# A hybrid decoder trunk: attention split into a projection phase and an interleaved attention, gate and output phase

## The chip, the cores and the metric

The kernel runs on one core of a Trainium2 chip. The metric is device time in microseconds (us) of one execution, median of several runs. The engines that matter are PE (TensorE: matrix products and transposes, results in PSUM), ACT (ScalarE: activations, copies), DVE (VectorE: element-wise work), POOL (GpSimd: the same, slower) and SP, whose queue issues nearly all DMA transfers. Each engine runs its own instruction list in order and waits on semaphores that other engines raise.

## What is computed

One inference step of two layers over 2048 prompt tokens and 8 sample tokens of width 1024. Layer A is a gated short convolution. Layer B is attention with its own queries against shared keys and values in three groups with (window, dilation) = (128,1), (512,4), (2048,16); 8 query heads and 2 key/value heads of width 128 per group.

```python
k, v = rope((rms_norm(x, g) @ w_kv)[keys]), (rms_norm(x, g) @ w_kv)[values]     # 3 groups x 2 heads
q, z = rope((rms_norm(x, pre) @ w_in)[: 3*8*128]), (rms_norm(x, pre) @ w_in)[3*8*128 :]
for g in range(3):                         # query t reads t - k*d, k = 0..window/d
    s = q[g] @ k[g].T * SCALE;  s = where(mask, s, -inf)
    lse[g] = logsumexp(s);      o[g] = exp(s - lse[g]) @ v[g]
alpha = softmax(lse over g)
o = sum(alpha[g] * o[g])
y = x + rms_norm((o * silu(z)) @ w_out, post)
```

With dilation d, the tokens t = r mod d form a sequence of their own. A tile is 128 query tokens of one such sequence. A query of it sees at most two blocks of 128 keys: its own and the one before. In the group with dilation 16 each sequence has just 128 tokens, so all 16 tiles have one block; in the middle group 4 of 16 have one; in the group with dilation 1 all are handled with two.

Single-precision products are made as three passes: each operand is split into a high part (a rounded copy, made by ACT) and a low part (the rest, a subtraction on DVE or POOL), and hi x hi + lo x hi + hi x lo are accumulated. A product over 1024 inputs into 512 columns thus takes 8 x 3 = 24 matmuls.

## The kernel before

`decoder_program` (L2257) runs four phases, each closed by a barrier.

1. **Convolution layer** (`conv_phases` L56 and its helpers): leaves the residual rows `h_rows` and the normalised rows `hn_rows` in DRAM. The change does not touch it.
2. **`attention_phase`** (L807), for each group in the order 0, 1, 2 and for each tile (`step`): the tile's 128 tokens are loaded in the order of the group and turned (8 transposes, with high and low parts by ACT `high` L1283 and DVE `low` L1385). They are the stationary operand of `project` (`product` L1120 to L1127): 3 banks of 512 columns (K and V, first four query heads, last four), 72 matmuls. DVE (L1409, L1410) and POOL (L1511) apply the rotary factors. Keys and queries are turned (`turn` L1110). For each half of the heads (two units a tile): `scores` (L1156 to L1158), mask and maximum on DVE (L1426, L1429), the exponent bias (L1434), `exponentials` on ACT (L1313), `turn_probs`, `values` (L1185 to L1187, the values stationary and the turned probabilities moving, 512 columns), a copy on ACT (L1321) and `turn_sums`. The function `between` places the next tile's projection in six spots of this one, so that PE has products to do while the other engines work. The 8 sample rows are projected once per group (`project_sample`). Each tile's sums, exponent bias and denominator go to DRAM as `partial`.
3. **`sample_attention_phase`** (L1551): the 8 sample tokens against the caches. Meanwhile 16 weight slices, of the gate's and of the output's matrix, are loaded and split and stay for the next phase.
4. **`attention_output_phase`** (L1880), for each token tile: tokens are loaded and turned again, the gate product (`d_z`, L2055 to L2057), Silu on ACT (L2122), merge coefficients (L2174 to L2188), `weigh` (L2147, two groups on POOL and one on DVE), sums and gating on DVE (L2200 to L2207), a turn of the gated rows, the output product (`d_out`, same lines), square sum, root (ACT L2109), `reciprocal_root` (L39) and normalising (L2163) on DVE, the residual sum on POOL (L2234).

The order of the work inside a phase is the order in which each engine's instructions are written out; there is no planner.

Of the kernel before, what the change touches and what calls it, by code (L numbers as in the profile page):

```python
# [22 lines left out]
P = 128  # L23
D = 1024
# [775 lines left out]
OMW = D + 2 * HEADS  # L800

Item = namedtuple("Item", "g i u last")


def attention_phase(nc, hn_rows, w_kv, w_q, kv_gain, q_gain, rope_rows,  # L807
                    partials, caches_out, q_sample, new_rows, newest):
# [4 lines left out]

    TILES = SEQ // P
    UN = 4
    BODIES = TILES // UN
    EACH = range(GROUPS)
    ITEMS = TILES + 1
    KW = KVW + KVW + D
    BANK_COLS = [slice(b * BANK, (b + 1) * BANK) for b in range(3)]

    def rows(w):

        step = DILATIONS[w.g]
        row_i, row_u = ((UN * P, P), (1, UN * P), (UN, 1))[w.g]
        return bass.ds(row_i * w.i + row_u * w.u, P, step=step)

    def ahead(w, k):


        u = w.u + k
        if not w.last or u < UN:
            return Item(w.g, w.i + u // UN, u % UN, w.last)  # L840
        if w.g == GROUPS - 1:
            return None
        return Item(w.g + 1, 0, None, False) if u == UN else Item(w.g + 1, 0, u - UN - 1, False)

    def exists(w, k):

        return not w.last or w.u + k < UN or w.g < GROUPS - 1

    def ordinal(w):

        return ITEMS * w.g + (0 if w.u is None else 1 + UN * w.i + w.u)

    def parity(w):

        return (ITEMS * w.g + (0 if w.u is None else 1 + w.u)) % 2

    def landed(w):

        return (ITEMS * w.g + (0 if w.u is None else 1 + w.u)) // 2 + (0 if w.u is None else UN // 2 * w.i) + 1

    def height(w):
        return NS if w.u is None else P

    def number(w):

        return TILES * w.g + UN * w.i + w.u

    def has_before(w):

        return w.g == 0 or (w.g == 1 and w.u > 0)  # L870

    def names(w):

        probs = ("a", "b") if has_before(w) else ("a",)
        tokens = ("h0", "h1") if exists(w, 2) else ()
        return ["q0", "k", "q1", *tokens, *("p0" + x for x in probs), *("p1" + x for x in probs), "o0", "o1"]

    per_body = [sum(len(names(Item(g, 0, u, False))) for u in range(UN)) for g in EACH]

    first_job = [6, 6 + BODIES * per_body[0] + 2, 6 + BODIES * (per_body[0] + per_body[1]) + 4]  # L880
    assert all(n % 2 == 0 for n in per_body)

    def job(w, name):

        before = sum(len(names(w._replace(u=v))) for v in range(w.u)) + names(w).index(name)
        return first_job[w.g] + before + per_body[w.g] * w.i, before % 2

    def run_steps(engine, g, step):

        with engine.Fori(0, BODIES - 1) as i:  # L890
            for u in range(UN):
                step(Item(g, i, u, False))
        for u in range(UN):
            step(Item(g, BODIES - 1, u, True))

    def sample(g):
        return Item(g, 0, None, False)

    def first(g, u):
        return Item(g, 0, u, False)  # L900

    with ExitStack() as ctx:
        def sb(name, shape, dt=F32):
            return ctx.enter_context(nc.sbuf_tensor(f"g_{name}", shape, dt))

        def ps(name, shape):
            return ctx.enter_context(nc.psum_tensor(f"g_{name}", shape, F32))

        def sem(name):
            return nc.alloc_semaphore(f"g_{name}")  # L910

        w_raw = [sb(f"w_raw{b}", [P, KW]) for b in range(2)]
        w_hi = sb("w_hi", [P, KT, KW], F32R)
        w_lo = sb("w_lo", [P, KT, KW], F32R)
        gains = sb("gains", [P, 2, KT])
        tok = [sb(f"tok{b}", [P, D]) for b in range(2)]
        ht_hi = [sb(f"ht_hi{b}", [P, KT, P], F32R) for b in range(2)]
        ht_lo = [sb(f"ht_lo{b}", [P, KT, P], F32R) for b in range(2)]
        trig = [sb(f"trig{b}", [P, 3, HD // 2]) for b in range(2)]
        rot_a = sb("rot_a", [P, 3, BANK])  # L920
        rot_b = sb("rot_b", [P, 3, BANK])

        raw = [w_raw[0][:], w_raw[1][:], *(x[:].rearrange("p b n -> p (b n)") for x in (rot_a, rot_b))]
        RAW = len(raw)
        q_rot = [sb(f"q_rot{n}", [P, BANK]) for n in range(KVH)]
        kv_rows = [sb(f"kv_rows{b}", [P, 2 * KVW]) for b in range(2)]
        qt_hi = [sb(f"qt_hi{n}", [P, BANK], F32R) for n in range(KVH)]
        qt_lo = [sb(f"qt_lo{n}", [P, BANK], F32R) for n in range(KVH)]
        kt_hi = sb("kt_hi", [P, KVH, 2 * P], F32R)
        kt_lo = sb("kt_lo", [P, KVH, 2 * P], F32R)  # L930
        v_hi = [sb(f"v_hi{b}", [P, KVW], F32R) for b in range(2)]
        v_lo = [sb(f"v_lo{b}", [P, KVW], F32R) for b in range(2)]
        probs = sb("probs", [P, QPK, 2 * P])
        pt_hi = sb("pt_hi", [P, 2 * BANK], F32R)
        pt_lo = sb("pt_lo", [P, 2 * BANK], F32R)
        sum_t = [sb(f"sum_t{n}", [P, BANK]) for n in range(KVH)]
        minus_max = sb("minus_max", [P, QPK])
        part = [sb(f"part{b}", [P, OMW]) for b in range(2)]
        mask_f = sb("mask_f", [P, 3, P])


        mask = sb("mask", [P, (3 + 2 * BODIES) * P], BF16)
        ident = sb("ident", [P, P])

        proj = ps("proj", [P, 3, BANK])
        score = ps("score", [P, QPK, 2 * P])
        tps = [ps(f"tps{b}", [P, BANK]) for b in range(2)]
        out_ps = ps("out", [P, BANK])
# [3 lines left out]
        s_mask = sem("mask_ready")  # L952
        s_wraw = [sem(f"w_landed{b}") for b in range(RAW)]
        s_whi = sem("w_hi_ready")
        s_wlo = sem("w_lo_ready")
        s_tok = [sem(f"tok_landed{b}") for b in range(2)]
        s_trig = [sem(f"trig_landed{b}") for b in range(2)]
        s_tr = sem("transposed")
        s_tr_hi = sem("transposed_hi")
        s_tr_free = sem("transpose_evacuated")  # L960
        s_proj = sem("projected")
        s_rope = sem("rope_products")
        s_rot = sem("rotated")
        s_v = sem("v_copied")
        s_vhi = sem("v_hi_ready")
        s_vlo = sem("v_lo_ready")
        s_score = sem("scores_ready")
        s_masked = sem("scores_masked")
        s_max = sem("max_ready")
        s_bias = sem("bias_ready")  # L970
        s_exp = sem("exps_ready")
        s_pv = sem("pv_ready")
        s_sum_t = sem("sums_t_copied")

        s_kvstore = [[sem(f"kv_stored{g}_{b}") for b in range(2)] for g in EACH]
        s_partstore = [sem(f"partial_stored{b}") for b in range(2)]
        s_sstore = sem("sample_stored")

# [9 lines left out]
        def kv_rows_stored(engine, w):  # L988

            if w.u is None:  # L990
                return
# [1344 lines left out]
```

## Time and profile before

| | us |
|---|---|
| median of three runs (2848.39 to 2852.35) | 2850.98 |
| the profiled execution, its own time | 2846.44 |
| its span in the trace | 2844.7 |
| mean granted PE clock, share of 2.4 GHz | 0.973 |
| PE, DVE, ACT, POOL busy | 2716.5, 1188.3, 974.2, 449.4 |
| convolution layer, first DMA of attention | 0 to 981.0 |
| attention phase, to the first DMA of the sample phase | 981.0 to 2343.2 |
| sample phase, to the first DMA of the output phase | 2343.2 to 2416.5 |
| output phase | 2416.5 to 2844.7 |

Times in the trace are us from the start of the span. In a timeline each line gives the start, the length, the engine, the line of the kernel, the operation, what it writes and reads, and in brackets how long the engine was idle before it and what released it. PE's durations overlap (a 512-column matmul is shown with 0.39 us though the next begins 0.23 us later), so PE's work is read from starts. PEclk is the clock that PE was granted, as a share of 2.4 GHz; 0.50 is its lower level, 1.2 GHz.

### The profile page before, as it was taken

To read this page: it belongs to the slowest core of one execution; us is meant where nothing else is said; L and a number is where in the kernel's file an instruction comes from. 1 tells how busy PE (TensorE), PEld (TensorE's weight loads), DVE (VectorE), ACT (ScalarE), POOL (GpSimd) and SP (SyncE) were. 2 spreads that over 40 slices of the span, in tenths; PEclk is the share of its full clock that TensorE was granted. 3 is DMA by queue.
4 is the path that set the end of the run, shared out by engine and by line. 5 is a ranking of instruction groups with operands and counts; after the bars stand their busy time and mean duration, and the time that the engine had idled before them with its cause. 6 is when DMAs were issued, how large, how long until landed. Compare 5 with 4: busy or idle time off the path is not lost. (4 is left out here: it accounts for less than half of the span.)

```text
span 2844.7 us, 39420 instructions
## 1 busy us (share of the span) xinstructions
PE 2716.5 (95%) x14124; PEld 2349.4 (83%) x14124; DVE 1188.3 (42%) x2208; ACT 974.2 (34%) x2163; POOL 449.4 (16%) x330
## 2 busy tenths in 40 slices
PE   6999999999999699999989999989999977999997
PEld 5999999999987478888858888867888867788885
DVE  7311111111334355555555455464444433455552
ACT  6211111111255434444343344353333333233332
POOL 1010110101022211111111111111111110233332
PEclk9999999999999899999999999999999985999999
DMA  4232323323555421111131111131111116433330
GB/s 150 91 104 71 110 95 107 96 79 125 172 174 176 158 78 41 49 41 40 56 112 42 46 44 49 39 128 52 52 60 60 56 40 204 170 134 134 134 120 31
DMA packets 128411, 264.49 MB, mean 93 GB/s; under 512 B 14125, under 2 KB 81541, under 8 KB 126794
## 3 DMA queue, kind: packets, MB, share of 16 engines
q1 hardware_dynamic: 122138, 219.41, 23.3%
q10 hardware_dynamic: 6192, 44.01, 4.7%
q8 instruction: 50, 0.82, 0.1%
q14 instruction: 31, 0.25, 0.0%
HBM read 198.21 MB, written 109.19 MB: 108 GB/s over the span
## 5 line engine op out<-in xcount | busy, mean ns | idle before, releaser
L1125 PE MATMUL g_proj<-g_w_hi,g_ht_hi 128*128 128x512 f32 (+1 forms) x1224 | 509.0, 416 | 21.1 <-DVE g_w_lo L1440 21.1
L1127 PE MATMUL g_proj<-g_w_hi,g_ht_lo 128*128 128x512 f32 (+1 forms) x1224 | 485.2, 396 | 0.0
L1126 PE MATMUL g_proj<-g_w_lo,g_ht_hi 128*128 128x512 f32 (+1 forms) x1224 | 485.0, 396 | 0.0
L280 PE MATMUL a_pair<-a_ht_hi,a_w_hi 128*128 128x412 f32 (+1 forms) x1280 | 448.5, 350 | 2.0 <-DVE a_ht_lo L449 2.0
L281 PE MATMUL a_pair<-a_ht_lo,a_w_hi 128*128 128x412 f32 (+1 forms) x1280 | 447.6, 350 | 0.0
L282 PE MATMUL a_pair<-a_ht_hi,a_w_lo 128*128 128x412 f32 (+1 forms) x1280 | 447.4, 350 | 0.0
L1125 PEld LDWEIGHTS g_proj<-g_w_hi,g_ht_hi 128*128 128x128 f32 (+1 forms) x1224 | 223.5, 183 | 75.0 <-DVE g_w_lo L1440 17.0
L1127 PEld LDWEIGHTS g_proj<-g_w_hi,g_ht_lo 128*128 128x128 f32 (+1 forms) x1224 | 223.2, 182 | 63.9 <-issue 2.6
L1126 PEld LDWEIGHTS g_proj<-g_w_lo,g_ht_hi 128*128 128x128 f32 (+1 forms) x1224 | 224.1, 183 | 49.0 <-issue 2.1
L280 PEld LDWEIGHTS a_pair<-a_ht_hi,a_w_hi 128*128 128x128 f32 x1280 | 241.2, 188 | 3.0 <-DVE a_ht_lo L449 2.4
L281 PEld LDWEIGHTS a_pair<-a_ht_lo,a_w_hi 128*128 128x128 f32 x1280 | 241.1, 188 | 1.0
L282 PEld LDWEIGHTS a_pair<-a_ht_hi,a_w_lo 128*128 128x128 f32 x1280 | 241.0, 188 | 0.6
L1511 POOL TENSOR_TENSOR g_q_rot<-g_rot_a,g_rot_b 128x512 f32<-128x512 f32 (+1 forms) x102 | 131.2, 1287 | 652.2 <-DVE g_rot_b L1410 652.2
L1313 ACT ACTIVATE g_probs<-g_score,g_part 128x256 f32<-128x256 f32 (+1 forms) x384 | 159.9, 429 | 113.9 <-DVE g_part L1434 113.9
L1426 DVE TENSOR_TENSOR g_score<-g_score,g_mask 128x1024 f32<-128x1024 f32 (+1 forms) x96 | 96.8, 1009 | 227.2 <-PE g_score L1158 227.1
L239 POOL TENSOR_TENSOR a_w_lo<-a_w_raw,a_w_hi 128x1024 fp32r<-128x1024 f32 x32 | 76.2, 2403 | 619.7 <-ACT a_w_hi L340 619.7
L1385 DVE TENSOR_TENSOR g_pt_lo<-g_tps,g_pt_hi 128x512 fp32r<-128x512 f32 x152 | 99.7, 687 | 119.5 <-ACT g_pt_hi L1283 119.5
L503 DVE TENSOR_TENSOR a_y<-a_pair,a_conved 128x412 f32<-128x412 f32 (+1 forms) x40 | 23.4, 586 | 281.0 <-ACT a_silu_z L362 281.0
L1321 ACT ACTIVATE g_sum_t<-g_out 128x512 f32<-128x512 f32 x96 | 57.4, 598 | 204.0 <-PE g_out L1187 204.0
L467 DVE TENSOR_TENSOR a_u<-a_c,a_pair 128x412 f32<-128x412 f32 (+1 forms) x40 | 23.3, 583 | 232.5 <-ACT a_c L344 232.5
L1156 PE MATMUL g_score<-g_kt_hi,g_qt_hi 128*128 128x256 f32 (+1 forms) x384 | 110.1, 287 | 5.8 <-ACT g_probs L1313 3.0
L362 ACT ACTIVATE a_silu_z<-a_pair 128x412 f32<-128x412 f32 (+1 forms) x40 | 20.6, 515 | 275.4 <-PE a_pair L282 275.2
(221 smaller groups left out, 4919.5 us busy)
## 6 DMA issues: line engine op xcount, KB each, us to landing
out_cache_kv_g_sample<-cache_kv_g ACTq DMA_DIRECT2D x72, 410.0 KB, 3.5
scratch_partial<-g_part SPq DMA_DIRECT2D x48, 520.0 KB, 2.9
d_part<-scratch_partial SPq DMA_DIRECT2D x48, 520.0 KB, 4.7
g_tok<-scratch_hn_rows SPq DMA_DIRECT2D x48, 512.0 KB
a_w_raw<-a_w_in SPq DMA_DIRECT2D x32, 512.0 KB, 5.3
a_x<-x_prompt SPq DMA_DIRECT2D x16, 512.0 KB, 3.6
b_y_raw<-scratch_y_t SPq DMA_DIRECT2D x16, 512.0 KB, 5.1
b_x<-x_prompt SPq DMA_DIRECT2D x16, 512.0 KB, 4.1
```

Source lines behind the costliest of these rows:

```text
L239: nc.gpsimd.tensor_tensor(w_lo[k][:], w_raw[k % 2][:], w_hi[k][:].bitcast(F32), ALU.subtract).then_inc(s_wlo, 1)
L280: nc.tensor.matmul(out, hi, ht_hi[:, k, cols], start=(k == 0), stop=False)
L281: nc.tensor.matmul(out, hi, ht_lo[:, k, cols], start=False, stop=False)
L282: last = nc.tensor.matmul(out, lo, ht_hi[:, k, cols], start=False, stop=(k == KT - 1))
L1125: nc.tensor.matmul(out, hi, w_hi[:, k, cols], start=(k == 0), stop=False)
L1126: nc.tensor.matmul(out, hi, w_lo[:, k, cols], start=False, stop=False)
L1127: last = nc.tensor.matmul(out, lo, w_hi[:, k, cols], start=False, stop=(k == KT - 1))
L1156: nc.tensor.matmul(out, qt_hi[n][:, q], kt_hi[:, n, cols], start=True, stop=False)
L1313: nc.scalar.activation(probs[:, h, cols], score[:, h, cols], ACT.Exp, bias=part[w.u % 2][:, D + x:D + x + 1], scale=SCALE, accum_out=part[ ...
L1385: nc.vector.tensor_tensor(lo, bank_view(at[1], width, hi), hi.bitcast(F32), ALU.subtract).then_inc(s_tr_free, 1)
L1426: nc.vector.tensor_tensor(score[:, :, cols], score[:, :, cols], m.unsqueeze(1).to_broadcast([P, QPK, width]), ALU.add).then_inc(s_masked, 1)
L1511: nc.gpsimd.tensor_tensor(dst[0:n, 0:heads * HD], rot_a[0:n, bank, 0:heads * HD], rot_b[0:n, bank, 0:heads * HD], ALU.add).then_inc(s_rot, 1)
```

## The change

Phases 2 to 4 become three others; the convolution layer stays.

- **`projection_phase`**: all 2056 tokens are turned once and stay on the chip (`ht_hi`, `ht_lo`). Keys and values are projected token tile by token tile, group by group (51 jobs of 24 matmuls), and stored to `kv_rows`. Queries are projected channel by channel: for each of 12 pairs of heads the weights are the stationary operand and the tokens move in five chunks of 416 columns (the last 392), so that queries come out already turned. DVE (`rotate`) and POOL apply the rotary factors by a table with one column per token, in the group's order; a pair's queries are stored to `q_tiles`. Turned tokens are stored to `ht_tiles`.
- **`sample_attention_phase`**: loads and splits only the gate's 8 weight slices; its queries arrive turned.
- **`attention_phase`** (new): 48 tiles in the order of groups 2, 1, 0, two units each. Per unit PE turns the probabilities, does the next unit's scores and this unit's values. The turned probabilities are now stationary and the values move (high and low side by side, 256 columns, and one of 128), so that sums needn't be turned back; ACT `copy_low` and DVE `add_sums` add the two halves. Mask and maximum are one custom DVE operation per head (`maximum`). In tiles 0 to 33 PE also does half a token tile of the gate product (`gate_product`, 12 matmuls a unit), and silu(z) = z / (1 + exp(-z)) is made with ACT `Exp`, POOL `plus_one`, and on DVE a reciprocal and a product (`gate`), stored to `silu_rows`. The output's weights are loaded and split in tiles 17 to 24 and 33 to 34. From tile 33 on (group 0, where the other groups' partials are complete) a token tile is merged per attention tile, and from tile 34 on PE does the output product of the one before (`out_product`, 24 matmuls a unit); three output products and the sample rows are left for the end.

The core of the diff, after the change; removed are the old `attention_phase` and `attention_output_phase` as described above.

```diff
+            with pe.Fori(0, ALL_PAIRS // 2) as i:
+                for u in range(2):
+                    pe.wait_ge(s_qlo, 2 * KT * i + KT * (u + 1))
+                    for c in range(NCH):
...
+                        for x in range(2):
+                            out = slot[:, x, 0:size[c]]
+                            for k in range(KT):
+                                hi, lo = q_hi[u][:, x, k, :], q_lo[u][:, x, k, :]
+                                nc.tensor.matmul(out, hi, ht_hi[:, k, cols], start=(k == 0), stop=False)
+                                nc.tensor.matmul(out, hi, ht_lo[:, k, cols], start=False, stop=False)
+                                last = nc.tensor.matmul(out, lo, ht_hi[:, k, cols], start=False, stop=(k == KT - 1))
+                        last.then_inc(s_q, 1)
...
+            for e in range(UNITS):
+                a, n = divmod(e, 2)
...
+                turn_probs(e)
+                if e + 1 < UNITS:
+                    scores(e + 1)
+                if n == 0 and a + 2 < TILES:
+                    turn_keys(a + 2)
+                values(e)
+                if a < Z_JOBS:
+                    gate_product(a, range(4 * n, 4 * n + 4))
+                j = out_after(a)
+                if j is not None:
+                    out_product(j, n, range(0, 6))
+                if n == 1 and merged_in(a) is not None:
+                    turn_gated(merged_in(a))
+                if j is not None:
+                    out_product(j, n, range(6, KT))
...
+            def gate(z):
+                n, e = z_height(z), gate_exp
+                dve.wait_ge(s_zone, z + 1)
+                nc.vector.reciprocal(e[0:n, :], e[0:n, :]).then_inc(s_zinv, 1)
...
+                dve.wait_ge(s_zinv, z + 1)
+                nc.vector.tensor_tensor(gate_out[z % 2][0:n, :], wide[z % 2][0:n, :], e[0:n, :],
+                                        ALU.mult).then_inc(s_zout, 1)
...
+            for e in range(UNITS):
+                a, n = divmod(e, 2)
+                probs_lo(e)
+                if n == 0 and merged_in(a) is not None:
+                    least(merged_in(a))
+                if e + 1 < UNITS:
+                    maximum(e + 1)
+                if n == 0 and a + 2 < TILES:
+                    keys_lo(a + 2)
+                if n == 0 and 1 <= a <= Z_JOBS:
+                    gate(a - 1)
+                if n == 0 and merged_in(a) is not None:
+                    coefficients(merged_in(a))
+                if n == 1 and merged_in(a) is not None:
+                    merge(merged_in(a))
+                    gated(merged_in(a))
+                add_sums(e)
+                if n == 0 and out_after(a - 1) is not None:
+                    normalise(out_after(a - 1))
+                if n == 1 and NT < a <= NT + KT:
+                    weights_lo(0, a - NT - 1)
+                if n == 1 and merged_in(a) is not None:
+                    gated_lo(merged_in(a))
```

`values(e)` on PE waits for `probs_lo(e)`; `turn_probs(e)` for the exponentials, and these for `maximum(e)` and the bias. `merged_in(a)` is the token tile merged in tile a (from 33), `out_after(a)` the one whose output product runs in it (from 34); UNITS is 96, Z_JOBS 34, NT 16.

## Rows read from the trace of the kernel before

**Rows 1.** Page, busy time of all engines: us (share of the span) xinstructions.

```profile
PE 2716.5 (95%) x14124; PEld 2349.4 (83%) x14124; DVE 1188.3 (42%) x2208; ACT 974.2 (34%) x2163; POOL 449.4 (16%) x330
```

**Rows 2.** Windows: start:end length, busy us of each engine, PEclk, DMA share, GB/s.

```profile
1100.00:1150.00 50.00, 50.00 (x269) 42.10 (x268) 26.00 (x43) 20.73 (x56) 7.35 (x7) 1.00 0.11 39
...
2300.00:2350.00 50.00, 30.69 (x157) 24.92 (x155) 15.78 (x30) 15.00 (x50) 4.52 (x6) 0.74 0.19 59
...
2350.00:2400.00 50.00, 45.70 (x208) 42.87 (x208) 18.63 (x26) 23.80 (x41) 0.00 (x0) 0.50 0.73 246
```

**Rows 3.** Timeline of PE, first query turn of four tiles: start, us, line, out<-in.

```profile
1200.25 0.60 PE L1110 MATMUL g_tps<-g_ident,g_q_rot 128*128 128x128 f32 x4
...
1227.32 0.60 PE L1110 MATMUL g_tps<-g_ident,g_q_rot 128*128 128x128 f32 x4
...
2104.78 0.63 PE L1110 MATMUL g_tps<-g_ident,g_q_rot 128*128 128x128 f32 x4
...
2129.38 0.63 PE L1110 MATMUL g_tps<-g_ident,g_q_rot 128*128 128x128 f32 x4
```

**Rows 4.** Timeline of PE: successive matmuls of 512 and of 256 columns, one of 128.

```profile
1201.38 0.39 PE L1125 MATMUL g_proj<-g_w_hi,g_ht_hi 128*128 128x512 f32 x1
...
1201.61 0.40 PE L1126 MATMUL g_proj<-g_w_lo,g_ht_hi 128*128 128x512 f32 x1
...
1226.01 0.28 PE L1157 MATMUL g_score<-g_kt_lo,g_qt_hi 128*128 128x256 f32 x1
...
1226.13 0.28 PE L1158 MATMUL g_score<-g_kt_hi,g_qt_lo 128*128 128x256 f32 x1
...
2129.27 0.28 PE L1158 MATMUL g_score<-g_kt_hi,g_qt_lo 128*128 128x128 f32 x1
```

**Rows 5.** Timelines of SP's queue and ACT; page, DMA issues: xcount, KB, us to landing.

```profile
981.03 0.29 SPq L1007 DMA_DIRECT2D g_tok<-scratch_hn_rows  x1
...
2339.27 0.33 SPq L1068 DMA_DIRECT2D scratch_partial<-g_part  x1
...
2343.18 0.40 SPq L1638 DMA_DIRECT2D s_cache<-cache_kv_g  x1
...
2416.48 0.33 SPq L1979 DMA_DIRECT2D d_tok<-scratch_hn_rows  x1
...
2835.58 0.97 ACT L2106 ACTIVATE d_square<-d_out 8x1024 f32<-8x1024 f32 x1 [15.06 <-PE d_out L2057]
...
d_part<-scratch_partial SPq DMA_DIRECT2D x48, 520.0 KB, 4.7
```

**Rows 6.** Grouped instructions: line, engine, out<-in xcount | busy us, mean ns | idle before.

```profile
L1385 DVE TENSOR_TENSOR g_pt_lo<-g_tps,g_pt_hi 128x512 fp32r<-128x512 f32 x152 | 99.7, 687 | 119.5 <-ACT g_pt_hi L1283 119.5
...
L2147 POOL TENSOR_TENSOR d_part<-d_part,d_coef 128x1024 f32<-128x1024 f32 x32 | 76.7, 2416 | 37.3 <-DVE d_coef L2188 37.3
...
L2163 DVE SCALAR_TENSOR_TENSOR d_normed<-d_out,d_stat,d_post_gain 128x1024 f32<-128x1024 f32 x16 | 20.5, 1284 | 0.8
```

**Rows 7.** One line's instructions: duration ns min/median/max, first and last start, forms.

```profile
L2186 DVE RECIPROCAL d_small<-d_small x16: 202/203/205, 2425.9 to 2780.4; 128x8 f32<-128x8 f32 x16
...
L45 DVE RECIPROCAL d_scratch<-d_stat x17: 141/152/154, 2469.1 to 2837.1; 128x1 f32<-128x1 f32 x16, 8x1 f32<-8x1 f32 x1
...
L1807 DVE CUSTOM_DVE_ANT_0 s_product<-s_q_rows,s_new x3: 282/283/284, 2354.3 to 2354.9; 64x128 f32<-64x128 f32 x3
```

**Rows 8.** Timeline of POOL and DVE in the output phase, last tile but some.

```profile
2518.49 2.39 POOL L2234 TENSOR_TENSOR d_h<-d_h,d_normed 128x1024 f32<-128x1024 f32 x1 [15.49 <-DVE d_normed L2163]
...
2518.53 2.39 DVE L2178 TENSOR_TENSOR d_coef<-d_small,d_part 128x24 f32<-128x24 f32 x1
```

**Rows 9.** Windows around the change from group 0 to 1, columns as in rows 2.

```profile
1437.00:1440.00 3.00, 1.26 (x9) 0.94 (x9) 1.87 (x4) 2.23 (x5) 2.00 (x2) 1.00 0.42 165
...
1440.00:1443.00 3.00, 2.48 (x12) 2.07 (x11) 1.31 (x2) 1.20 (x2) 0.00 (x0) 0.50 0.88 274
...
1461.00:1464.00 3.00, 1.78 (x11) 0.68 (x9) 2.77 (x3) 3.00 (x6) 0.00 (x0) 1.00 0.02 6
```

More of the change, by code:

```diff
@@ L800 @@
 OMW = D + 2 * HEADS
[L804 to L900, printed above, removed]
-    with ExitStack() as ctx:
-        def sb(name, shape, dt=F32):
-            return ctx.enter_context(nc.sbuf_tensor(f"g_{name}", shape, dt))
@@ L917, in attention_phase @@
[L917 to L926, printed above, removed]
@@ L936, in attention_phase @@
[L936 to L946, printed above, removed]
+            return nc.alloc_semaphore(f"p_{name}")
+        ht_hi = place("ht_hi", [P, KT, TOK], F32R, base)
@@ L1913, in attention_output_phase @@
         scratch = sb("scratch", [P, 3])
[L1914 to L1918 removed]
+        gate_out = [out_sb[:, x * BANK:(x + 1) * BANK] for x in range(2)]
+        gate_exp = normed[:, 0:BANK]
+        score = ps("score", [P, QPK, 2 * P])
+        sums = ps("sums", [P, QPK, 2, HD])
         tps = [ps(f"tps{b}", [P, BANK]) for b in range(2)]
[L1921 removed]
+        wide = [ps(f"wide{b}", [P, BANK]) for b in range(2)]
@@ new lines, in exponentials @@
+            def exponentials(e):
+                a, n = divmod(e, 2)
+                width = 2 * P if full(a) else P
+                act.wait_ge(s_bias, e + 1)
+                if e >= 1:
+                    act.wait_ge(s_pt, 2 * e)
+                for h in range(QPK):
+                    x = QPK * n + h
+                    nc.scalar.activation(probs[:, h, 0:width], score[:, h, 0:width], ACT.Exp,
+                                         bias=parts[a % 2][:, 0, D + x:D + x + 1], scale=SCALE,
+                                         accum_out=parts[a % 2][:, 0, D + HEADS + x:D + HEADS + x + 1])\
+                      .then_inc(s_exp, 1)
@@ L2144, in weigh @@
+            last = out_after(TILES - 1)
+            copy_out(last, 1)
+            merge_exps(NT - 1)
+            squares(last)
+            root(last)
+            for j in range(last + 1, OUT_JOBS):
+                copy_out(j, 0)
+                if j + 1 < OUT_JOBS:
+                    gated_hi(j + 1)
+                copy_out(j, 1)
+                squares(j)
+                root(j)
         def weigh(engine, b, g):
-            x = part[b][:, g, 0:D].rearrange("p (h d) -> p h d", d=HD)
+            x = parts[b][:, g, 0:D].rearrange("p (h d) -> p h d", d=HD)
```

1861 lines of the change are left out of this document (1072 added, 789 removed).

## The prediction

> **What bounds the kernel now.** I read the page's busy times first, then the table of windows, then PE's timeline, then the grouped instructions. PE is busy for 2716.5 of 2844.7 us, every other engine for under half [rows 1]. Inside the attention phase PE is full: 50.00 of 50 us at clock 1.00 between 1100 and 1150 [rows 2]. PE's order there is one instruction list, so a tile lasts as long as its matmuls: the turns of a group's queries start at 1200.25 and again at 1227.32, 27.07 us later, for a tile with two key blocks, and at 2104.78 and 2129.38, 24.60 us, for a tile with one [rows 3]. The steps between starts give the price of PE work: 0.23 us for a 512-column matmul (0.2333 over a whole tile), 0.12 for 256 columns [rows 4], 0.11 for 128 (2129.27 to 2129.38 [rows 3, 4]) and, as the check shows, for a transpose. Check: 72 projections and 12 value matmuls at 0.2333, 24 score matmuls at 0.119 and 42 transposes at 0.11 give 27.08. The filler runs out only at the ends: 30.69 of 50 us from 2300 to 2350, and the sample phase after it runs at clock 0.50 [rows 2]. So now the bound is PE work. The question is whether the changed kernel can still keep PE fed.
>
> **What the change does to PE work.** The K/V products stay: 51 jobs (17 token tiles, three groups) of 24 matmuls, 5.6 us each, 285.6 us. Tokens are turned once instead of three times and once more for the gate. Queries become 60 jobs of 48 matmuls: 12 head pairs, four chunks of 416 columns and one of 392. At 0.2333/512 = 0.456 ns a column that is 0.190 and 0.179 us, so 12 x 48 x (4 x 0.190 + 0.179) = 540 us; before it was 51 x 48 x 0.2333 = 571, because the 8 sample rows cost full passes. In attention, query turns (8 a tile) go, and sums are not turned back (8). A full tile is now: keys turned 0.22, scores 24 x 0.119 = 2.86, probabilities turned 1.76, values 16 x (0.119 + 0.111) = 3.68, together 8.5 us; a one-block tile 5.6. Before, without projection and token turns, these were 9.4 and 6.9. Gate and output products stay at 34 x 5.6 = 190 us each; half of the gate's job is now spread over each of 34 tiles, the output's 11.2 us over each of the last 14. PE gives back about 31 (queries) + 51 (attention tiles) + 45 (token turns) us, and some 25 us at the changes of group. Were PE full throughout, the span would be near 2690.
>
> **The timeline, stage by stage.** I don't take 2690, because the new order puts other engines on PE's path.
> *Projection.* It starts where attention started, at 981.0 [rows 5]. First tile ready about 994.5 (estimate: tokens and first weights land in some 5 us, as a load of this size does [rows 5], then turns, two splits and the first weights' low part). Group 0 takes 16 x (5.6 + 0.88) = 104, groups 1 and 2 95 each and 2 for the first weights: 1290. Queries 540: 1830. DVE has four operations of some 0.6 us a job, plus weight splitting, of 9.1 us; POOL two adds of 1 us: both hidden, and four times too much would be needed to show. Last rotation, adds, a 2 MB store and the barrier (the last store before was issued at 2339.27 and the next phase began at 2343.18 [rows 5]): 12.5, so 1842.
> *Sample phase.* It lost half of its weight slices, but PE was busy 45.70 of 50 us in it at half clock [rows 2]: the length stays at 2416.5 - 2343.2 = 73 [rows 5], so 1915.
> *Attention start.* POOL makes the first low parts of queries and then the masks, in this order; its 1024-wide operation takes 2.4 us [rows 6]. Landing 5 [rows 5], two splits 6, masks 2, first maxima and exponentials 4: 17, so 1932.
> *Tiles with gate work (0 to 33).* DVE's list has, ahead of add_sums(e) and probs_lo(e+1), the function gate: a reciprocal of 128x512 and a product. Behind it waits values(e+1) on PE, and behind that in PE's list everything else. No reciprocal of this width is in the trace. A 128x8 one takes 203 ns, a 128x1 one 152 [rows 7]: 7.3 ns for each further element, 3.9 us for 512. The lower bound is a plain 512-wide pass at 0.69 [rows 6], the upper one 512 x 203/8 = 13 us; I take 3.9, the slope between rows of the same operation. By the Trainium skill ("VectorE: DVE Perf Modes", section "First, the fixed hardware budget") reciprocal is an iterative divide with a repeat count of 8; with the 0.96 GHz of the same page my estimate from it is 4.3 us, which would add 13 us to the sum. The loop from one tile's first scores to the next tile's: maxima four times 0.5 (a custom operation of 128 elements takes 0.283, three of them start 0.3 apart [rows 7]) and the bias 0.1; keys_lo 0.43; reciprocal R; product 0.69; add_sums 0.69; half of probs_lo 0.65; then on PE values 1.84, gate 2.8, turns 0.88, scores 1.43; and 0.3 between engines: 11.8 + R = 15.7 against 14.1 of PE work. A one-block tile: 9.8 + R = 13.7 against 11.7. So 20 x 13.7 + 12 x 15.7 = 462 for tiles 0 to 31. Tiles 32 to 34, where w_out's second half is split and the merge begins: 16 + 24 + 31 = 71 (estimate).
> *Tiles 35 to 47.* PE work 8.5 + 11.2 + 0.9 = 20.6. DVE has some 19 us of work a tile, and normalise (1.28 us [rows 6]) waits for a root on ACT with a table load; laid side by side by hand the lists give 23.3. On top, weighing, merging, gating and normalising take both inputs from SBUF while POOL works 10 us of the tile (two weights at 2.4, an add, a split [rows 6]). The one collision of this kind I can show turned a 0.18 us subtraction into 2.39, exactly as long as POOL's add beside it [rows 8]. I take 1 us of it a tile: 24.3, ends 20.6 and 27. 13 x 24.3 = 316.
> *Tail.* Three output products of 11.2 and the last chain. From the last square at 2835.58 the old one had 9 us to the end [rows 5]; with copies 13. Sum 47.
> Total 1932 + 462 + 71 + 316 + 47 = 2828, plus the 1.7 us that the profiled execution has around its span: 2830, against 2846.4. The median of the runs lies 4.5 us above that execution, so I forecast **2834 us** against 2851, 0.6% faster. Little is left of 150 us, because 100 of them turn into waits on DVE and the rest into start-up.
>
> **Transfers.** Queries go out and come back through DRAM: 5.2 MB each way per pair and table in 45 us of products, under what the trace has moved (246 GB/s at a share of 0.73 from 2350 to 2400 [rows 2]). I cost them at nothing; if a pair's tables came late at each pair, 12 x 6 = 72 us.
>
> **Rivals.**
> *A, PE stays full (faster).* If R is 1.9 or less, or its place in the list hurts less, tiles 0 to 31 fall to 20 x 11.7 + 12 x 14.1 = 403, and without collisions 13 us more go: 2834 - 59 - 13 = 2762. For it: a width of 8 may be a poor guide to 512. Against it: the sixteen 128x8 rows lie within 3 ns, all above those of 128x1.
> *B, the clock falls (slower).* In every gate tile PE would stand idle about 2 us between scores and values. Before, PE was never without filler there. When PE worked 1.26 of 3 us with idle times of under 1 us, the clock was 0.50 in the next window; with 1.78 of 3 us it stayed at 1.00 [rows 9]. A gate tile has PE busy 85%, which speaks against B. If the clock falls nonetheless, 2 us of matmuls cost 2 us more in each of 32 tiles: +55 or so, 2890. It decides from 0.5 us a tile, where the 17 us of gain are gone. The Trainium skill ("TensorE: Matmul & The Clock Gate", Part 1) says that the throttled state is the default and activity releases it; that rule speaks for B, the rows with short idle times against it.
> *C, collisions in the last third (slower).* At 27 us a tile and with two more in tiles 33 and 34: +38, 2872.
> *D, the projection isn't fed (slower).* The change would not give PE its shorter work: late tables, 2906.
>
> **How the numbers follow.** Forecast 0.48, A 0.22, B 0.15, C 0.10, D 0.05. The forecast's own range is 2800 to 2868 (R between 3.2 and 4.4: -20 to +15, group 0 at 23 or 25: 17, start-ups 10). 0.2%, 5.7 us, is about what a measurement of this kernel tells from no change. Of the forecast 0.35 lies below 2845, 0.05 within, 0.08 above. Faster 0.35 + 0.22 = 0.57, same 0.05, slower 0.08 + 0.30 = 0.38. The range takes in A's 2762 with its spread and B's 2890, and leaves out D and the far ends: 2745 to 2895.
>
> **What would show it.** In the profile after: the query products solid at clock 1.00 for 540 us and 0.19 us apart; a reciprocal of 3.9 us on DVE; in each gate tile one idle time of 1.5 to 2 us on PE, released by DVE's probs_lo; period 13.7 (one block) and 15.7 (two blocks); 24 us in the last tiles. It is wrong if the reciprocal is far from 3.9, if the clock row shows 0.5 inside tiles, or if PE waits for a transfer in the query jobs.

## The result and the profile after

The changed kernel takes 2816.58 us (median of four runs, 2816.27 to 2821.81) against 2849.68 beside it: a ratio of 0.9887 with an interval of 0.9870 to 0.9904, 33 us less. The forecast was 2834. The range held the time and the sign was right; the gain is about twice what was forecast.

The page after: busy time, and the granted clock in 40 slices.

```profile
PE 2613.9 (93%) x14140; PEld 2381.3 (85%) x14140; DVE 1291.2 (46%) x2821; ACT 876.7 (31%) x2025; POOL 638.7 (23%) x440
PEclk9999999999999899999999999956999999899999
```

PE works 103 us less than before [rows 1], but the span is only 29.9 us shorter: 73 of the 103 us have become idle time of PE. The stages, from timelines of SP's queue and of PE (start, length, engine, line; in brackets the idle time before and its end):

```profile
978.37 0.36 SPq L944 DMA_DIRECT2D p_tok<-scratch_hn_rows  x1
...
1289.38 0.35 PE L1118 MATMUL p_pair<-p_ht_hi,p_q_hi 128*128 128x416 f32 x1
1289.57 0.35 PE L1119 MATMUL p_pair<-p_ht_lo,p_q_hi 128*128 128x416 f32 x1
...
1828.23 0.34 PE L1120 MATMUL p_pair<-p_ht_hi,p_q_lo 128*128 128x392 f32 x1
...
1834.17 0.59 SPq L1011 DMA_DIRECT2D scratch_q_tiles<-p_q_out  x1
...
1843.57 0.70 SPq L1013 DMA_DIRECT2D scratch_q_sample<-p_q_out  x1
...
1849.05 0.38 SPq L1398 DMA_DIRECT2D s_cache<-cache_kv_g  x1
...
1923.19 0.33 SPq L1804 DMA_DIRECT2D g_q_raw<-scratch_q_tiles  x1
...
1938.69 1.12 PE L1977 MATMUL g_tps<-g_ident,g_probs 128*128 128x128 f32 x4 [4.72 <-ACT g_probs L2110]
```

They answer to [rows 4] and [rows 5]: a query matmul every 0.19 us, without a gap, from 1289.38 to 1828.4, 539 us where 540 were forecast. From there to the sample phase it is 20.6 us, not 12.5: SP issues the last pair's eight stores from 1834.17 to 1844.27. The sample phase's 74 us are as forecast. Attention reaches its first turn 6.7 us later than the forecast said.

From then on a tile is read from the start of the turn of its keys (line 1930). Lengths in us, from the differences of these starts, in the profiled executions:

| kernel | tile with one block (2 to 15) | tiles 17 to 31, mean | tiles 0 to 31 | 32, 33, 34 | 35 to 44, mean | 35 to the end |
|---|---|---|---|---|---|---|
| forecast | 13.7 | 15.3 | 462 | 16, 24, 31 | 24.3 | 363 |
| after | 12.83 | 14.52 | 437.5 | 14.8, 26.1, 31.6 | 24.69 | 362.7 |

What I read of a gate tile (timeline of DVE and PE, tile 7):

```profile
2034.36 0.25 DVE L2269 TENSOR_SCALAR g_parts<-g_maxima 128x4 f32<-128x4 f32 x1
...
2034.77 3.35 DVE L2297 RECIPROCAL g_normed<-g_normed 128x512 f32<-128x512 f32 x1
...
2038.22 0.69 DVE L2301 TENSOR_TENSOR g_out_sb<-g_wide,g_normed 128x512 f32<-128x512 f32 x1
...
2038.83 0.68 DVE L2289 TENSOR_TENSOR g_parts<-g_sums,g_low_sums 128x512 f32<-128x512 f32 x1
...
2039.42 0.68 DVE L2281 TENSOR_TENSOR g_pt_lo<-g_tps,g_pt_hi 128x512 fp32r<-128x512 f32 x1
...
2040.25 0.36 PE L1993 MATMUL g_sums<-g_v,g_pt_hi 128*128 128x256 f32 x1 [0.93 <-DVE g_pt_lo L2281]
```

This is the chain that the forecast described, in its order: reciprocal, product, add_sums, probs_lo, and PE's value products behind it. Only its length differs: the reciprocal takes 3.34 us, the idle time 0.93.

### The profile page after: what moved, and what is told of

Read it like the earlier page. It is cut to its first block and busy times, and to the rows that moved or that the text cites. A ratio compares the mean times of both kernels' runs of the same rounds, so it can differ in the third digit from the quotient of the medians.

```text
span 2814.8 us, 38189 instructions
## 1 busy us (share of the span) xinstructions
PE 2613.9 (93%) x14140; PEld 2381.3 (85%) x14140; DVE 1291.2 (46%) x2821; ACT 876.7 (31%) x2025; POOL 638.7 (23%) x440
## 5 line engine op out<-in xcount | busy, mean ns | idle before, releaser
L1118 PE MATMUL p_pair<-p_ht_hi,p_q_hi 128*128 128x416 f32 (+1 forms) x960 | 335.7, 350 | 0.0
L1119 PE MATMUL p_pair<-p_ht_lo,p_q_hi 128*128 128x416 f32 (+1 forms) x960 | 335.5, 350 | 0.0
L1120 PE MATMUL p_pair<-p_ht_hi,p_q_lo 128*128 128x416 f32 (+1 forms) x960 | 334.3, 348 | 0.0
L2110 ACT ACTIVATE g_probs<-g_score,g_parts 128x256 f32<-128x256 f32 (+1 forms) x384 | 159.9, 429 | 159.1 <-DVE g_parts L2269 159.1
L1118 PEld LDWEIGHTS p_pair<-p_ht_hi,p_q_hi 128*128 128x128 f32 x960 | 180.1, 188 | 2.4 <-DVE p_turned L1249 0.4
L1120 PEld LDWEIGHTS p_pair<-p_ht_hi,p_q_lo 128*128 128x128 f32 x960 | 180.5, 188 | 1.6
L1119 PEld LDWEIGHTS p_pair<-p_ht_lo,p_q_hi 128*128 128x128 f32 x960 | 180.2, 188 | 1.1
L1082 PE MATMUL p_pair<-p_w_hi,p_ht_hi 128*128 128x512 f32 (+1 forms) x408 | 163.9, 402 | 5.0 <-DVE p_w_lo L1200 5.0
L1993 PEld LDWEIGHTS g_sums<-g_v,g_pt_hi 128*128 128x128 f32 x608 | 116.0, 191 | 54.0 <-issue 27.2
L1084 PE MATMUL p_pair<-p_w_hi,p_ht_lo 128*128 128x512 f32 (+1 forms) x408 | 161.3, 395 | 0.0
L1083 PE MATMUL p_pair<-p_w_lo,p_ht_hi 128*128 128x512 f32 (+1 forms) x408 | 160.9, 394 | 0.0
## 6 DMA issues: line engine op xcount, KB each, us to landing
p_table<-rope_columns SPq DMA_DIRECT2D x60, 416.0 KB, 3.2
```

Source lines behind the costliest of these rows:

```text
L1082: nc.tensor.matmul(out, hi, w_hi[g % 2][:, k, :], start=(k == 0), stop=False)
L1083: nc.tensor.matmul(out, hi, w_lo[g % 2][:, k, :], start=False, stop=False)
L1084: last = nc.tensor.matmul(out, lo, w_hi[g % 2][:, k, :], start=False, stop=(k == KT - 1))
L1118: nc.tensor.matmul(out, hi, ht_hi[:, k, cols], start=(k == 0), stop=False)
L1119: nc.tensor.matmul(out, hi, ht_lo[:, k, cols], start=False, stop=False)
L1120: last = nc.tensor.matmul(out, lo, ht_hi[:, k, cols], start=False, stop=(k == KT - 1))
```

## The experiments

Theory: in tiles 0 to 33 the reciprocal stands on PE's path, and its length sets the tile. Rivals: another step is late right behind it; the clock falls when PE idles. Later a second theory came in, on what holds DVE in the last third.

**1. A cheap operation in place of the reciprocal.**

```diff
-                nc.vector.reciprocal(e[0:n, :], e[0:n, :]).then_inc(s_zinv, 1)
+                nc.vector.tensor_scalar(e[0:n, :], e[0:n, :], 1.0, None, ALU.mult).then_inc(s_zinv, 1)
```

> The changed kernel with the 128x512 reciprocal replaced by a multiplication by 1.0 of the same tile in place; silu(z) is then not what it should be, the work around it is the same. Theory (the reciprocal stands on PE's path in each gate tile): the idle time of PE in front of the value products goes, 0.9 us in a one-block tile and some 0.6 in a two-block one, so tiles fall from 12.82 to about 11.9 and from 14.8 to about 14.1, and the time by 24 to 30 us, to about 2790. Rival (something else is late right behind it, such as the copy of the low sums or the exponentials): under 10 us.

Measured: 2798.1 in a single run, 18 us less: under the 24 to 30 of the theory and over the 10 of the rival. Two-block tiles fell to 14.14, their PE work (between 2320 and 2370 PE waited 0.2 us in all), but one-block tiles only from 12.83 to 12.69. Half of the gain came where I had not looked: tiles 33 and 34, where the reciprocal lies beside weight splitting and merging, took 47.9 us instead of 57.8. So the reciprocal is on the path, and in one-block tiles something else stands right behind it (experiments 8 and 9).

**2. Two reciprocals**, and **3. one and a half.**

```diff
                 nc.vector.reciprocal(e[0:n, :], e[0:n, :]).then_inc(s_zinv, 1)
+                dve.wait_ge(s_zinv, 2 * z + 1)
+                nc.vector.reciprocal(e[0:n, :], e[0:n, :]).then_inc(s_zinv, 1)   # in 3: columns 0 to 255 alone
...
-                dve.wait_ge(s_zinv, z + 1)
+                dve.wait_ge(s_zinv, 2 * z + 2)
```

> The changed kernel with a second reciprocal of the same tile behind the first; silu(z) is then not what it should be. Theory: each tile already waits for DVE's list, so all of 34 x 3.34 = 114 us shows, about 2930. Rival (the list has slack, the wait at the value products comes from elsewhere): clearly less, under 80 us. Rival on the clock: with PE idle over 4 us a tile the granted clock falls to 0.50 inside tiles and the time rises by more than 114 us.

> The changed kernel with half a reciprocal more (256 of the 512 columns a second time, 1.74 us) in each gate job; silu(z) is then not what it should be. PE's idle time in front of the value products would be some 2.7 us a tile. Theory without the clock: 34 x 1.74 = 59 us, about 2876. Theory with the clock (it falls to half in tiles where PE idles that long, as with the second whole reciprocal, where 114 us of work cost 197): 90 to 105 us, about 2915, with a granted clock under 0.9 in the gate tiles.

Measured: 3013.5 and 2924.6, one run each, that is 197 us for 114 us of DVE work and 108 for 60. Here the clock falls: over the gate tiles it was 0.83 (1960 to 2564) and 0.90 (1959 to 2479) on average, against 1.00 in the changed kernel (1955 to 2394). Windows of the one-and-a-half kernel around one idle time (columns as in rows 2):

```profile
2053.00:2056.00 3.00, 3.00 (x20) 2.54 (x19) 2.97 (x2) 1.51 (x7) 0.00 (x0) 1.00 0.74 285
2056.00:2059.00 3.00, 0.88 (x8) 0.74 (x7) 2.90 (x4) 1.54 (x3) 1.69 (x1) 0.97 0.01 1
2059.00:2062.00 3.00, 2.40 (x10) 2.33 (x11) 1.63 (x10) 1.23 (x7) 1.35 (x2) 0.50 0.63 225
2062.00:2065.00 3.00, 3.00 (x9) 2.33 (x8) 0.69 (x1) 0.77 (x3) 0.00 (x0) 0.50 0.34 124
```

and of the changed kernel:

```profile
2036.00:2039.00 3.00, 3.00 (x22) 2.65 (x21) 2.90 (x3) 1.51 (x5) 0.00 (x0) 1.00 0.74 282
2039.00:2042.00 3.00, 2.07 (x15) 1.82 (x15) 2.89 (x11) 0.97 (x2) 2.25 (x1) 1.00 0.31 122
2042.00:2045.00 3.00, 3.00 (x20) 2.54 (x18) 0.85 (x2) 2.25 (x10) 0.83 (x2) 1.00 0.61 198
```

After an idle time of 2.7 us PE runs the gate product at 0.50; after 0.9 us it stays at 1.00. So rival B's mechanism is real on this kernel, and it did not strike in tiles 1 to 32 of the changed kernel, where the shorter reciprocal left an idle time of 0.9 us.

**4. The forecast's own reciprocal.** The edit of 3 with 68 columns the second time: 3.34 + 0.58 = 3.92 us.

> The changed kernel with 68 columns of the reciprocal a second time (some 0.56 us), so that the reciprocal takes the 3.9 us of the forecast; silu(z) is then not what it should be. If the clock stays up with PE idle 1.5 us a tile, the forecast's tiles come out, 13.4 and 15.4 us, and 19 us more than 2816, about 2835, which is the forecast: then its miss is the reciprocal's size. If the clock falls in some tiles as it did with 2.7 us of idle time, 2845 or more.

Measured: 2843.9 (eight runs, 2835.6 to 2848.1), ratio 0.9973 (0.9958 to 0.9988). Undisturbed tiles took 13.44 and 15.40; PE's idle time was 1.5 us in a one-block tile and 1.0 to 1.4 us in a two-block one, and in the trace 5 of the 30 tiles behind the first two (two of the first kind, three of the second) were 1.5 us longer, with a stretch at half clock in them:

```profile
2027.00:2030.00 3.00, 1.48 (x14) 1.34 (x13) 2.86 (x6) 1.85 (x3) 1.08 (x1) 0.97 0.17 65
2030.00:2033.00 3.00, 2.97 (x11) 2.81 (x12) 1.20 (x9) 1.66 (x9) 1.96 (x2) 0.50 0.34 95
```

Over the eight runs time and mean clock go together: 2835.6 us at 0.968, 2848.1 at 0.964. Tiles 0 to 31 together: 463.2 us, where the forecast had 462. That these two meet is luck: the forecast's even tiles are 0.3 us too long at this reciprocal, some 10 us in 32, and the clock, which it left out, took 7.5 us in five of them. So with the reciprocal as long as I put it, the change would have gained 5 us by the medians, 8 by the ratio. My expectation gave the two outcomes as alternatives; it was something between them, some tiles with and most without.

**5. silu by tanh**, z(1 + tanh(z/2))/2, the 0.5 in the gating product.

```diff
-                nc.scalar.activation(gate_exp[0:n, :], wide[z % 2][0:n, :], ACT.Exp, scale=-1.0)
+                nc.scalar.activation(gate_exp[0:n, :], wide[z % 2][0:n, :], ACT.Tanh, scale=0.5)
...
-                nc.vector.reciprocal(e[0:n, :], e[0:n, :]).then_inc(s_zinv, 1)
-                nc.vector.tensor_tensor(gate_out[z % 2][0:n, :], wide[z % 2][0:n, :], e[0:n, :], ALU.mult)
+                nc.vector.scalar_tensor_tensor(out=gate_out[z % 2][0:n, :], in0=e[0:n, :], scalar=1.0,
+                                               in1=wide[z % 2][0:n, :], op0=ALU.add, op1=ALU.mult)
...
-                nc.vector.tensor_tensor(x, x, silu_z[j % 2][0:n, :], ALU.mult)
+                nc.vector.scalar_tensor_tensor(out=x, in0=x, scalar=0.5, in1=silu_z[j % 2][0:n, :], op0=ALU.mult, op1=ALU.mult)
```

> silu(z) made without a reciprocal: ACT makes tanh(z/2), DVE one scalar_tensor_tensor (t + 1) * z out of PSUM, the factor 0.5 goes into the gating product; POOL's addition of 1 goes. Theory: as with a cheap reciprocal, 24 to 32 us less, about 2788. Rival (a table load for each change between exponential and tanh, 2 x 1.28 us a tile on ACT ahead of the exponentials): the gain is gone, 2810 or more.

Measured: 2799.4 (0.9818, 0.9802 to 0.9835), 11 us above what I expected and the same as the cheap operation in the gate tiles (12.69, 14.04 on average; tiles 33 and 34 together 45.4 for 47.9). No table load stands in the gate tiles of either kernel's trace. That agrees with the Trainium skill ("ScalarE: Activation LUTs", section "Table sets: the hidden batching unit"), which lists tanh in the set of the exponential.

**6. The reciprocal in two halves**, one in each unit of the tile; **7. the same with the store of silu(z) a tile later in SP's list.**

```diff
-                if n == 0 and 1 <= a <= Z_JOBS:
-                    gate(a - 1)
+                if 1 <= a <= Z_JOBS:
+                    gate(a - 1, n)                 # 256 columns each
...
-                if 1 <= a <= Z_JOBS:               # 7, SP
-                    store_gate(a - 1)
+                if 2 <= a <= Z_JOBS + 1:
+                    store_gate(a - 2)
```

> The same arithmetic as the changed kernel, with the reciprocal and its product cut into two halves of 256 columns, one in each of the tile's two units. Theory (what hurts is 3.34 + 0.69 us in one unit's list, while the other unit's list has room): most of the 24 to 30 us come back, about 2795. Rival (the sum of DVE's work in a tile is what counts, wherever it stands): within 6 us of 2816.

> The halves of before, with the store of silu(z) put one tile later in SP's list. Theory (halving helped the tiles, but SP, which waits for the second half, held the loads and the store of the partial sums back, and DVE waited up to 3.1 us for that store): one-block tiles at 12.7 again, time about 2797. Rival (the halves themselves cost that, by DVE's work in the second unit): 2820 or more again.

Measured: 2828.4 (0.9923), 12 us *slower* than one whole reciprocal, and 2809.8 (0.9865), 7 us faster. Two-block tiles came down to 14.14 in both, as the theory said, but with 6 one-block tiles were uneven, 13.29 on average. The cause stands in the waits of that kernel between 2000 and 2140 (who waited for whom, us in total, times, longest):

```profile
DVE g_parts L2269 <- DMA scratch_partial<-g_parts: 17.5, 9, 3.1
```

SP waited for the second half, and the four loads behind this wait, 1.8 MB together, were then issued in one go right ahead of the store of the partial sums. With the store of silu(z) later the one-block tiles are at 12.68. The halves don't reach the tanh version because tiles 33 and 34 keep their length (24.3 and 30.9). My rival on DVE's total work is out by the tiles, which fell to 12.68 and 14.14 with the same work on DVE; the time alone, 7 us less where the rival allowed 6, would hardly show it. The expected 2797 missed that the two-tile loss stays.

**8. POOL's split out of the way in the last third.** What the changed kernel shows in tile 41 (start 2600.48; POOL's split of the next queries, then DVE's bias, the two merging sums, the gating's end as PE's wait):

```profile
2613.22 2.40 POOL L2426 TENSOR_TENSOR g_qt_lo<-g_q_raw,g_qt_hi 128x1024 fp32r<-128x1024 f32 x1
...
2613.51 2.14 DVE L2269 TENSOR_SCALAR g_parts<-g_maxima 128x4 f32<-128x4 f32 x1
...
2615.56 1.21 DVE L2344 TENSOR_TENSOR g_parts<-g_parts 128x1024 f32<-128x1024 f32 x1
2615.58 1.80 POOL L2429 TENSOR_TENSOR g_v<-g_kv_raw,g_v 128x256 fp32r<-128x256 f32 x1
...
2616.81 1.65 DVE L2346 TENSOR_TENSOR g_parts<-g_parts 128x1024 f32<-128x1024 f32 x1
...
2619.77 1.09 PE L2048 MATMUL g_tps<-g_ident,g_parts 128*128 128x128 f32 x8 [2.00 <-DVE g_parts L2355]
```

```diff
                 if a + 2 < TILES:
+                    if merged_in(a) is not None:
+                        pool.wait_ge(s_gated, merged_in(a) + 1)
                     split_lo(a + 2)
```

> The changed kernel with one wait more: from tile 33 on POOL starts the low parts of the next queries and values (2.4 + 0.74 us) only after DVE has gated the tile, so that they no longer lie beside DVE's bias and merging sums. Theory (in the last third POOL's split holds DVE: the bias took 2.14 us instead of 0.17 and the sums behind it start late, PE then waits 2.0 us for the gated rows): tiles 35 to 47 fall from 24.6 to about 22.5, 24 to 28 us in all, to about 2791. Rival (the length of DVE's own list sets these tiles, or POOL now comes late with the queries): within 6 us of 2816.

Measured: 2785.3 (0.9778, 0.9762 to 0.9795), 31 us less for one wait. The same place there:

```profile
2569.13 0.17 DVE L2269 TENSOR_SCALAR g_parts<-g_maxima 128x4 f32<-128x4 f32 x1
2569.21 1.22 DVE L2344 TENSOR_TENSOR g_parts<-g_parts 128x1024 f32<-128x1024 f32 x1
2570.46 1.22 DVE L2346 TENSOR_TENSOR g_parts<-g_parts 128x1024 f32<-128x1024 f32 x1
...
2573.03 2.40 POOL L2426 TENSOR_TENSOR g_qt_lo<-g_q_raw,g_qt_hi 128x1024 fp32r<-128x1024 f32 x1 [4.13 <-DVE g_parts L2355]
...
2573.23 1.03 PE L2048 MATMUL g_tps<-g_ident,g_parts 128*128 128x128 f32 x8
```

The bias is back at 0.17 us, the sums at 1.22, PE's wait is gone; tiles 35 to 44 take 22.15 instead of 24.69, and 33 and 34 together 51.3 instead of 57.8.

**9. tanh with POOL's split moved everywhere** (behind the bias in tiles 0 to 32, behind the gating from 33 on).

> silu(z) by tanh, without reciprocal, and POOL's split in every tile moved to where DVE doesn't need it: behind the bias in tiles 0 to 32, behind the gating from tile 33. Theory (what stays behind the reciprocal is the same collision: the bias takes 0.9 to 1.5 us beside POOL's split in the second unit): one-block tiles from 12.67 to about 12.3, 7 us, and the last third 24 to 28 us: about 2767. Rival (the collision isn't on the path): 2795 or more.

Measured: 2779.7 (0.9763): the last third as in 8, but one-block tiles between 12.2 and 15.5, 13.64 on average. Not my expectation and not the rival: the wait moved on. Waits between 2000 and 2140, and the page's time to landing of the store that is waited for (xcount, KB, us):

```profile
DVE g_parts L2269 <- DMA scratch_partial<-g_parts: 19.4, 9, 4.2
...
scratch_partial<-g_parts SPq DMA_DIRECT2D x32, 520.0 KB, 8.4
```

A tile's bias goes into the buffer whose sums, of two tiles before, are still on their way out. At 12.3 us a tile the store must be through in time; it is queued behind four loads of 1.8 MB together (the expectations below count 1.3).

**10. Loads behind the store** in SP's list, on top of 9; **11.** the same on top of 8, with the reciprocal kept.

```diff
                 if 1 <= a <= LAST:
                     store_part(a - 1)
+                if a >= 1:
+                    load_tile(a + 3)
+                    if a + 1 < Z_JOBS:
+                        load_rows(a + 1)
...
-                load_tile(a + 4)
-                if a + 2 < Z_JOBS:
-                    load_rows(a + 2)
```

> The tanh kernel with POOL's split moved, and in SP's list the loads of the next tiles (1.3 MB) put behind the store of the partial sums instead of ahead of it. Theory (in group 2 the bias of a tile waits up to 4.2 us for the store of the partials two tiles earlier, which is queued behind those loads and lands 8.4 us after its issue): one-block tiles 12.3 all through instead of 12.2 to 15.5, some 20 us less than 2780, about 2760. Rival (the store is slow by its own pattern of rows 16 apart, or the loads now come late): within 6 us of 2780.

> The changed kernel, reciprocal kept, with POOL's split behind the gating from tile 33 and the loads behind the store. Theory (with the reciprocal in the list the store of the partials was never the last to come, tiles were even at 12.82): within 4 us of the 2785 that the moved split gave, so that the reciprocal's whole price, once the waits behind it are removed, is about 25 us. Rival (the order of loads is a gain by itself): 2778 or less.

Measured: 2756.3 (0.9678, 0.9663 to 0.9693) and 2786.2 (0.9781). The store lands in

```profile
scratch_partial<-g_parts SPq DMA_DIRECT2D x32, 520.0 KB, 3.0
```

and the one-block tiles are even at 12.24 (the longest 12.52). With the reciprocal kept the same order of loads brings nothing: tiles of 12.83 did not wait for the store before either. Between 11 and 10 lie 2786.2 - 2756.3 = 30 us; in experiment 5, with the waits behind the reciprocal in place, taking it out brought 17. The 30 us are not the reciprocal's alone, though: 11 leaves POOL's split of tiles 0 to 32 beside DVE's bias, 10 moves it too. A kernel that keeps the reciprocal and moves the split in those tiles was not run, so what each of the two is worth there stays open.

**12. The last stores from two queues**, on top of 10: ACT issues half of the last pair's stores.

> The kernel with the loads behind the store, and the last pair's query stores issued half by SP and half by ACT. Theory (between the last query product and the sample phase lie 21 us, of which SP's issuing of eight stores takes 10): 5 us less than the run beside it. Rival (the landing, not the issue, sets the end): within 1.5 us of it.

Measured: 2755.8 (2749.0 to 2758.2), no difference that these runs can tell. In the trace the two queues are done with issuing at 1838.2 and 1839.0, counted from the last query matmul (1826.92) 4 us earlier than in the changed kernel, but the sample phase (1846.33) follows that matmul after 19.4 us, where it was 20.8 counted alike. What SP waits for at the end (us in total, times, longest), in the changed kernel and here:

```profile
SPq L1058 <- DMA scratch_q_sample<-p_q_out: 3.5, 1, 3.5
...
SPq L1061 <- DMA scratch_q_sample<-p_q_out: 6.9, 1, 6.9
```

Issued earlier, the stores took longer to land: the landing sets the end, not the issue, and the expectation was wrong.

The best version is that of experiment 10: 2756 us against 2847 before, 3.2% less, with the same arithmetic but for tanh. The tiles of all kernels (column names as in the table above):

| kernel | one block | 17 to 31 | 0 to 31 | 32, 33, 34 | 35 to 44 |
|---|---|---|---|---|---|
| 1 cheap operation | 12.69 | 14.04 | 427.8 | 14.1, 23.1, 24.8 | 24.58 |
| 2 two reciprocals | 18.37 | 20.58 | 618.3 | 20.6, 28.0, 34.6 | 24.57 |
| 3 one and a half | 15.90 | 17.83 | 536.2 | 19.6, 27.2, 32.7 | 24.57 |
| 4 forecast's reciprocal | 13.64 | 15.42 | 463.2 | 15.4, 26.7, 31.7 | 24.59 |
| 5 tanh | 12.69 | 14.04 | 428.3 | 14.1, 22.4, 23.0 | 24.62 |
| 6 halves | 13.29 | 14.30 | 440.2 | 14.1, 29.8, 31.2 | 24.93 |
| 7 halves, store later | 12.68 | 14.04 | 428.5 | 14.1, 24.3, 30.9 | 24.74 |
| 8 split moved | 12.83 | 14.53 | 437.3 | 14.8, 22.9, 28.4 | 22.15 |
| 9 tanh and split moved | 13.64 | 13.96 | 440.4 | 14.1, 19.0, 23.1 | 22.16 |
| 10 and loads behind | 12.25 | 13.77 | 416.0 | 14.1, 19.0, 23.2 | 22.15 |
| 11 as 8, loads behind | 12.83 | 14.53 | 437.0 | 14.8, 22.4, 28.7 | 22.15 |
| 12 as 10, two queues | 12.25 | 13.76 | 416.4 | 14.1, 19.0, 23.2 | 22.16 |

## Why the prediction was right or wrong

**PE work and the query phase: right.** 539 us for 540. PE waited for no transfer there, so rival D is out; DVE did wait for the tables, 26 times and up to 10.9 us, under PE's cover. K/V and tokens took 311 us (978.4 to 1289.4) for 309.

**The mechanism in the gate tiles: right; its size: wrong.** The step that failed is the reciprocal's price, 3.9 us, a slope from 1 and 8 columns. One line of the profile after (duration min/median/max, first and last start):

```profile
L2297 DVE RECIPROCAL g_normed<-g_normed x34: 3329/3343/3347, 1957.8 to 2422.7; 128x512 f32<-128x512 f32 x32, 8x512 f32<-8x512 f32 x2
```

And the second reciprocal, of 256 columns in experiment 3 and of 68 in experiment 4:

```profile
L2299 DVE RECIPROCAL g_normed<-g_normed x34: 1741/1753/1754, 1962.0 to 2532.1; 128x256 f32<-128x256 f32 x32, 8x256 f32<-8x256 f32 x2
...
L2299 DVE RECIPROCAL g_normed<-g_normed x34: 566/578/579, 1960.3 to 2452.5; 128x68 f32<-128x68 f32 x32, 8x68 f32<-8x68 f32 x2
```

With 0.153 us for one column that is 6.2 ns for each further one, not 7.3. The estimate of 4.3 us that the prediction worked out from the Trainium skill ("VectorE: DVE Perf Modes", section "First, the fixed hardware budget") was further off; the measurement decides. Experiment 4 puts the size of this one term on the chip: 2843.9 - 2816.6 = 27 us for 0.58 us of reciprocal. That is more than 34 x 0.58 = 20, because some tiles lose the clock as well (five in the trace, 1.5 us each).

**The sum, term by term** (own times, measured less forecast): first turn +6.7, of which the last stores +8.1 and the rest of the start the other way; tiles 0 to 31 -24.5; tiles 32 to 34 +1.6; the rest +3.0 (tiles 24.7 for 24.3, a shorter tail; it holds the 3.4 us from the first turn of probabilities, where the forecast starts its tiles, to the first turn of keys, where the tables do). Together -13.2: 2816.6 for 2829.7. Of the -24.5, 18 are the reciprocal's 0.56 us in 32 tiles; the loop's other pieces were 0.3 us too dear in an even tile, some 10 us in all, of which uneven tiles took 4 back. The last 4.5 us of the miss is a step that had no ground: I added the distance between the median of the runs and the profiled execution of before to the forecast; after, the two are equal (2816.58 and 2816.55).

**Rival A** (PE stays full) gave 2762 for a reciprocal of 1.9 us or less and no collisions. Experiment 1 had 0.42 us in its place and took 2798: two-block tiles came to the 14.1 of rival A, one-block tiles stayed 1 us above its 11.7, with the collisions and the store behind the reciprocal. 2756 was reached only with these removed too, and that it lies near 2762 is chance: tiles 0 to 31 took 416 us for 403, and the last third 22.15 us a tile for 23.3. (The 11.7 itself is a slip: the prediction's own 5.6 + 5.6 make 11.2. In experiment 10 PE was idle for 0.7 us of a 12.24 us tile, so its work there is 11.6.)

**Rival B** (the clock) did not occur in tiles 1 to 32, but the busy share of 85% that I set against it was no ground: with the reciprocal of 3.92 us that I had counted on, the clock fell in experiment 4. What the runs show is an idle time in each turn that grows with the reciprocal: with 0.9 us no tile at half clock, with 1.0 to 1.5 us some, with 2.2 to 2.7 us most, and with 4.3 us (experiment 2) one-block tiles of 18.4 us instead of the 16.2 that the longer list alone would make. With my own 3.9 us the forecast should have held a part of it. In tiles 33 and 34 the clock did fall in the changed kernel as well, which neither the forecast nor rival B had; their windows, columns as in rows 2:

```profile
2394.34:2420.47 26.13, 17.98 (x109) 13.77 (x108) 24.18 (x46) 12.50 (x33) 11.43 (x6) 0.87 0.37 137
2420.47:2452.11 31.64, 23.89 (x133) 20.79 (x132) 25.86 (x41) 12.90 (x34) 9.44 (x5) 0.84 0.41 145
```

**The last third: the total right, its make-up unseen.** 24.7 for 24.3. Rival C's 27 did not come. I priced collisions of DVE and POOL at 1 us a tile for operations with two inputs from SBUF. The runs show 2.5 us a tile (experiment 8), and that the first victim is the bias, a `tensor_scalar` with one input, which never took more than 0.172 us before:

```profile
L1434 DVE TENSOR_SCALAR g_part<-g_minus_max x96: 169/170/172, 1040.6 to 2330.1; 128x4 f32<-128x4 f32 x96
```

The Trainium skill ("SBUF — State Buffer", section "Who interferes with whom") names `tensor_scalar` among the operations that can, under conditions, take the port pair that DVE and POOL share, and says that the order of issue decides who waits; the rows of experiment 8 agree (POOL first at 2613.22, bias done at 2615.65), and I had overlooked it. By the rows of experiment 8 the bias makes 1.97 of the 2.5 us and the second merging sum 0.43 (1.65 for 1.22); the two were not tried apart.

**What stays open.** Why the tiles with half clock in experiment 4 are those five and not others; what the reciprocal and what POOL's split costs in the gate tiles once the store is out of the way; and what of the unchanged convolution layer's end (978.4 here, 981.0 before, 974 to 980 in the other runs) is chance.

## What to carry to other kernels

When work is moved under the matrix engine, list for each engine what stands *ahead* of the operation that the matrix engine waits for next; making one long element-wise operation there longer costs the whole difference in every turn, and more if the idle time takes the clock down, while making it shorter gains only what the next wait in line leaves (here 0.14 us of 2.9 in a one-block tile). An operation without a row of its own size deserves its own measurement, or a range that spans the forecast's sign: here 0.6 us of a reciprocal decided between 1.1% and 0.3%. After removing a wait, look who is late next: in the gate tiles the store of partials held DVE up once the reciprocal was gone and POOL's split moved, and the order of loads, worth 23 us then, brought nothing while the reciprocal stood.

## What of the hardware was unexpected

- A 128x512 reciprocal takes 3.343 us, a 128x256 one 1.753, a 128x68 one 0.578: 6.2 ns for each further column, where 8 columns against 1 suggested 7.3.
- A DVE `tensor_scalar` of 4 columns with one SBUF input was held for 2.14 us by a POOL subtraction of 1024 columns beside it (0.17 us in the kernel before and, with the subtraction moved, in experiment 8).
- The granted clock fell to 0.50 inside tiles in which PE had one longer idle time and worked on for the rest: 1.0 to 1.5 us in experiment 4 (5 of 30 tiles), 2.2 to 2.7 us in experiment 3 (most tiles). In experiment 3, 48 of the 108 us are not explained by the 60 us of added work; the clock accounts for them.
- A 520 KB store whose landing took 3.0 us when issued ahead of 1.8 MB of loads (experiment 10) took 8.4 behind them (experiment 9).
